# The inverse root's guess in the norms from logarithm and exponential, with a table load placed by hand

## What is computed

```python
def rms_norm(x, g):
    xf = x.astype(jnp.float32)
    y = xf * lax.rsqrt(jnp.mean(xf * xf, axis=-1, keepdims=True) + EPS)
    return (y * g.astype(jnp.float32)).astype(x.dtype)

def mixer_block(h, ...):
    xn = rms_norm(h, norm1_g)
    proj = xn @ w_in                      # fq fk fv ff cq ckv krope sq sk sv gates
    fq, fk = rms_norm(fq per head, fox_q_g), rms_norm(fk per head, fox_k_g)
    log_decay = jnp.cumsum(jax.nn.log_sigmoid(ff + fox_forget_b), axis=1)
    out_a = causal_block_attention(fq, fk, fv, log_decay)
    q = rms_norm(rms_norm(cq, mla_q_a_g) @ mla_w_q_up, mla_q_g)      # then rope
    kv = rms_norm(ckv, mla_kv_a_g) @ mla_w_kv_up
    k = rms_norm(k of kv and krope, mla_k_g)                         # then rope
    out_b = causal_block_attention(q, k, v_mla)
    sq, sk = rms_norm(sq per head, swa_q_g), rms_norm(sk per head, swa_k_g)
    out_c = sliding_window_attention(sq, sk, sv, swa_sinks, slopes)
    merged = sum over branches of sigmoid(gates) * (branch @ w_branch)
    return h + merged @ w_o

def conv_ffn(h, norm2_g, w_up, conv_w, conv_b, w_down):
    u = rms_norm(h, norm2_g) @ w_up       # convolution over 3 positions: gate, val
    return h + (jax.nn.silu(gate) * val) @ w_down
```

## Time and profile before

| | before |
|---|---|
| median of 3 runs | 2309.89 us |
| the profiled execution | 2311.74 us |
| its span | 2309.6 us |
| PE busy | 2064.9 us, 89% |
| DVE busy | 1293.0 us, 56% |
| ACT busy | 683.7 us, 30% |
| POOL busy | 882.9 us, 38% |

### The profile page before, as it was taken

One profiled execution on the slowest core, in us unless ns is written; L12 is line 12 of the kernel. 1 busy time (PEld: TensorE's weight loads), 2 busy tenths in 40 slices (PEclk: granted clock), 3 DMA queues, 4 the chain that ended last, 5 costly groups with the idle time before them and its releaser, 6 DMA issues.

```text
span 2309.6 us, 36668 instructions
## 1 busy us (share of the span) xinstructions
PE 2064.9 (89%) x15052; PEld 1945.4 (84%) x15052; DVE 1293.0 (56%) x2300; ACT 683.7 (30%) x1221; POOL 882.9 (38%) x494
## 2 busy tenths in 40 slices
PE   4999877878889999999979998878788899999999
PEld 3888776777779999999968887767777799999999
DVE  7565656466646565562266656564666565666511
ACT  3434332433331222220024343324343322222200
POOL 6444332232333344444464444322223334444443
PEclk9999988889889999999989999888898999999999
DMA  3111110111113333223221111111111132333333
GB/s 127 47 54 57 55 37 28 37 37 47 46 46 102 92 92 87 88 91 97 88 91 56 56 49 54 37 28 37 38 45 46 46 111 85 95 97 92 93 100 92
DMA packets 44794, 156.27 MB, mean 68 GB/s; under 512 B 5010, under 2 KB 5266, under 8 KB 44628
## 3 DMA queue, kind: packets, MB, share of 16 engines
q1 hardware_dynamic: 44484, 153.71, 22.2%
q10 hardware_dynamic: 144, 0.22, 0.0%
HBM read 149.58 MB, written 4.26 MB: 67 GB/s over the span
## 4 chain that ended last, share of the span: by engine, by line
PE 72%; DVE 18%; issue 5%; ACT 3%; POOL 1%; DMA 0%; DVEq 0%; ACTq 0%; POOLq 0%
PE ps L1156 20%; PE ps L1159 19%; PE ps L1161 19%; PE ps L1364 4%; PE ps L1166 3%; DVE osum L1731 2%; DVE rstd L1447 2%; PE ps L1312 1%; DVE ps L1701 1%; PE ps L1274 1%; DVE guess L1443 1%; DVE yq L1602 1%; DVE wh L1428 1%; DVE q L1575 1%; PE ps L1318 1%
## 5 line engine op out<-in xcount | busy, mean ns | idle before, releaser
L773 POOL TENSOR_TENSOR wl<-raw,wh 128x1024 fp32r<-128x1024 f32 x270 | 648.0, 2400 | 911.9 <-DVE wh L1428 905.9
L1156 PE MATMUL ps<-xh,wh 128*128 128x264 f32 (+1 forms) x2880 | 830.2, 309 | 35.8 <-DVE xl L1506 16.2
L1159 PE MATMUL ps<-xl,wh 128*128 128x264 f32 (+1 forms) x2880 | 781.9, 291 | 0.0
L1156 PEld LDWEIGHTS ps<-xh,wh 128*128 128x128 f32 x2880 | 564.1, 196 | 60.4 <-DVE xl L1506 18.9
L1161 PE MATMUL ps<-xh,wl 128*128 128x264 f32 (+1 forms) x2880 | 596.8, 289 | 0.0
L1159 PEld LDWEIGHTS ps<-xl,wh 128*128 128x128 f32 x2880 | 563.9, 196 | 13.1 <-issue 5.0
L1161 PEld LDWEIGHTS ps<-xh,wl 128*128 128x128 f32 x2880 | 463.7, 195 | 0.0
L1428 DVE CAST wh<-raw 128x1024 fp32r<-128x1024 f32 x270 | 199.9, 741 | 188.8 <-PE ps L1156 170.4
L1723 DVE TENSOR_TENSOR ps<-ps,cst 128x128 f32<-128x128 f32 (+6 forms) x240 | 69.6, 295 | 239.4 <-PE ps L1318 163.5
L1159 PE MATMUL ps<-al,wh 128*128 128x264 f32 (+1 forms) x704 | 185.0, 283 | 0.0
L1156 PE MATMUL ps<-ah,wh 128*128 128x264 f32 (+1 forms) x704 | 183.6, 283 | 0.0
(11 more groups left out here) (174 smaller groups left out, 3300.7 us busy)
## 6 DMA issues: line engine op xcount, KB each, us to landing
raw<-weights SPq DMA_DIRECT2D x270, 512.0 KB, 3.6
h<-tokens SPq DMA_DIRECT2D x4, 528.0 KB, 6.0
h<-tokens SPq DMA_DIRECT2D x8, 264.0 KB, 5.3
residual<-h SPq DMA_DIRECT2D x8, 264.0 KB, 4.7
h<-residual SPq DMA_DIRECT2D x8, 264.0 KB, 5.1
out<-h SPq DMA_DIRECT2D x8, 256.0 KB, 4.8
cst<-constants SPq DMA_DIRECT2D x1, 1008.0 KB
extra<-positions SPq DMA_DIRECT2D x17, 4.1 KB
```

Source lines behind the costliest of these rows:

```text
L773: nc.gpsimd.tensor_tensor(wl[c % SPLIT][:, :], raw[:, c % RAW, :], wh[c % SPLIT][:, :].bitcast(F32), ALU.subtract).then_inc(s_lo, 1)
L1156: a = nc.tensor.matmul(out, a_hi, x_hi[:, sl], start=first, stop=False)
L1159: nc.tensor.matmul(out, a_hi, x_lo[:, sl], start=False, stop=False)
```

## The change

The guess is no longer one function. Ln of the mean plus epsilon is taken, then Exp of -0.5 times that, then the Square as before: one ACTIVATE and one wait more per norm. A flag, `table["now"]`, follows which table is loaded as the program is written: `logarithms()` asks by name for the table that holds both Ln and Exp if the flag doesn't say so already, and it is called at the start of `rsqrt_guess` (behind the waits of lines 1016, 1017, 959 to 961, 1117 and 1118) and ahead of the decay's Exp. The flag is cleared at each Tanh and behind norm 2, since Silu follows. In front of Tanh and Silu the compiler puts its loads as before.

```diff
+            table = {"now": None}
+
+            def logarithms():
+
+                if table["now"] != "ln":
+                    nc.scalar.preload_act_table_set("natural_log_exp_and_others")
+                    table["now"] = "ln"
+
+            def follows(ins):
+
+                ins.then_inc(act_step.sem, act_step.tick(("a", act_step.n)))
+                act.wait_ge(act_step.sem, act_step.n)
+
             def rsqrt_guess(slot, n):
-                nc.scalar.activation(guess[:, :], full(slot), ACT.Abs_reciprocal_sqrt, scale=1.0 / n,
-                                     bias=epsb[:, 0:1]).then_inc(act_step.sem, act_step.tick(("a", act_step.n)))
-                act.wait_ge(act_step.sem, act_step.n)
+                logarithms()
+                follows(nc.scalar.activation(guess2[:, :], full(slot), ACT.Ln, scale=1.0 / n, bias=epsb[:, 0:1]))
+                follows(nc.scalar.activation(guess[:, :], guess2[:, :], ACT.Exp, scale=-0.5))
                 return nc.scalar.activation(guess2[:, :], guess[:, :], ACT.Square)
...
                             act.wait_ge(act_step.sem, act_step.at("f", l, 0))
+                            logarithms()
                             nc.scalar.activation(fe, fa, ACT.Exp, scale=-1.0).then_inc(
...
+                            table["now"] = None
                             nc.scalar.activation(gate_tile(t.m), full(t.slot), ACT.Tanh, scale=0.5).then_inc(
...
                 rsqrt_guess(1, D).then_inc(guess_ready.sem, guess_ready.tick((l, "n2")))
+                table["now"] = None
```

## The result

The changed kernel takes 2323.72 us, the median of 5 runs (2318.20 to 2326.82); the kernel before, timed beside it, 2308.85 us. The ratio is 1.0059, 95% interval 1.0040 to 1.0078: slower by 14 us (9 to 18). The forecast was 2329 in a range of 2312 to 2342. The profiled execution after is 2318.55 us with a span of 2316.4, so 6.8 us over the one profiled before. It is one of the two shortest of the five, which is why it shows less than the medians do.

The account below looks back on a forecast made before the run. PE was taken as the bound (busy 89% of the span, 72% of the chain). Terms of 9.5 us per layer, 19.0 in all, plus 0.7 once each made 19.7, taken as 19 on 2309.9: 2329 us, range 2312 to 2342.

Parts of the forecast that it names:

- Rival A: At the norms, the explicit load stays ahead of the wait for the statistic: 2313 us; chance 0.13.
- rival B: In the attention stages ACT's queue decides and its total counts: -11.4 us in all, 2298 us; chance 0.08.
- rival C: At the 58 norms the compiler's own loads still come behind the explicit one: some 50 us, 2360; chance 0.02.
- the terms for Fox, the sliding window and norm 1: Per layer: sliding-window shift rows +2.0, Fox queries 2 and 3 +1.1, Fox query 1 -0.3; layer 1's norm 1 +1.95.
- The terms for MLA: Per layer: query 1 -0.6, key 0 +0.65, queries 5 to 7 together +0.6, key 3 +1.95 us.
- MLA key 3: In each layer DVE waits for this key's guess and goes on to PE's scores: +1.95 us.
- terms put at nothing: Norm 2 of both layers, MLA keys 1 and 2, fewer loads ahead of exponentials elsewhere: all costed at nothing.
- The third term put at nothing: Fewer loads ahead of exponentials elsewhere: costed at nothing, as PE doesn't wait there.
- The Tanh term: Three Tanh loads per layer, at 449.56 and two more places: +1.28, 0.7 and 0.8, together +2.8 us per layer.
- The decay term: Decay of layer 1: two loads on the chain vanish, 2.57; query 0's guess takes back 0.67: -1.9 us.
- Link and spared loads: Extra Exp: 0.67 us from statistic to guess per norm, 37.4 us of ACT; 38 fewer loads: 48.8 us of ACT less.
- The signs I named: Profile after: 36 explicit loads, 34 Tanh loads, 58 Exp, ACT near 672 us, PE idle some +19, more DVE waits.

Follow-up runs that it names:

- e1: The changed kernel with the explicit table load asked for ahead of the waits for the statistic: 2307.85 us, ratio 0.9995 against the kernel before.
- e3: The kernel before with its own 54 norm loads made explicit and so put behind the waits, no additional link: 2341.27 us, ratio 1.0131.
- e10: The changed kernel with the load ahead of the waits, except in MLA's queries and keys and the layer's second norm: 2316.64 us, ratio 1.0032.
- e11: The changed kernel with the load ahead of the waits only in MLA's queries and keys and the second norm: 2313.68 us, ratio 1.0021.
- e4: The changed kernel with the gates' Tanh replaced by a Copy, so the 34 Tanh loads vanish: 2323.59 us, ratio 1.0059 against the kernel before.
- e5: The kernel before with the decay's Exp and Ln table named ahead of its wait, and the first guess's table at the start: 2311.96 us, ratio 1.0012.
- e6: e1 with the guess's Ln taken away, Exp reading the sum of squares directly (values wrong): 2296.43 us, ratio 0.9946 against the kernel before.
- e2: The kernel before with one additional Copy activation in the guess's chain, tables and loads untouched: 2331.25 us, ratio 1.0097.
- e8: e1 with Tanh's table asked for ahead of a score tile's wait (only 12 of 34 loads moved), first table at the start: 2309.86 us, ratio 1.0001.
- e9: e1 without the Square and Newton step, VectorE only scaling the guess from Ln and Exp: 2253.31 us, ratio 0.9763 against the kernel before.
- e12: The kernel before, with its old guess, without the Square and Newton step, VectorE only scaling the guess: 2238.62 us, ratio 0.9691.

## Why the prediction held, and which of its terms did not

**The direction and the mechanism held.** The load written behind both waits waits with them: the rows of line 948, e1 and e3 show it. Rival A (the load runs ahead), rival B (ACT's total decides, 2298) and rival C (more loads) are out for the changed kernel. e1 is rival A built on purpose. It was 2313 by my sum and measured 2307.85.

**The size of the place.** Rival A's terms add up to 5.3 us, which I rounded to 5, so between them and my forecast's sum lie 14.4 us, all from where the load stands. Measured: 14.8 (e1 against the changed kernel, 10 to 20). By place, the terms for Fox, the sliding window and norm 1 make (2.0 + 1.1 + 0.3) x 2 + 1.3 = 8.1, and e10 gave 6.2. The terms for MLA make (1.25 + 0.6 + 1.28) x 2 = 6.3, and e11, which has norm 2 as well, gave 8.8. Both differences are within the noise of the two runs. The step at sliding-window query 0 can be read directly. PE's timeline of the changed kernel, as the earlier trace rows:

```profile
230.06 0.18 PE L1328 MATMUL ps<-xq,xk 97*16 97x16 f32 x1 [1.05 <-ACT xq L941]
```

PE waits 1.05 us for the copied row, where I took 1.0. MLA key 3 held too: DVE waited 4.65 us for the guess before, 6.86 after. DVE's timeline of the changed kernel:

```profile
660.79 0.71 DVE L1459 SCALAR_TENSOR_TENSOR guess<-ps,guess 128x528 f32<-128x528 f32 x1 [6.86 <-ACT guess L960]
```

It reaches PE, which waits for that key. PE's timeline before and after:

```profile
666.44 0.36 PE L1274 MATMUL ps<-xk,xq 96*128 96x264 f32 x1 [3.22 <-DVE xk L1641]
```

```profile
667.31 0.56 PE L1290 MATMUL ps<-xk,xq 96*128 96x264 f32 x1 [5.31 <-DVE xk L1657]
```

That is 2.09 more where I took 1.95.

**Two of the terms put at nothing held.** At norm 2 of layer 0 DVE's wait for the guess grows from 4.73 to 6.68 us, the whole 1.95, but PE doesn't notice: from 780 to 796 us it is busy for all 16.00 in both kernels. At MLA key 2 the guess is late by 1.56 us, and the cover of the earlier trace rows gives way for it. DVE's second Newton instruction in the changed kernel:

```profile
590.50 0.75 DVE L1463 SCALAR_TENSOR_TENSOR rstd<-guess,guess 128x528 f32<-128x528 f32 x1
```

It starts later and takes 0.75 us instead of 2.39, and ends at 591.25, where it ended at 592.07 before. The first norm's +0.67 was swallowed in the same way: its second Newton instruction ends at 19.21 in both kernels (18.05 and 1.16 before, 18.50 and 0.71 after). The third term put at nothing, the loads spared ahead of exponentials, failed; it stands below.

**The Tanh term failed at the end, though not in the waits.** I took 2.8 us per layer, 5.6 in all, for three Tanh loads in line. The waits are there: PE's wait behind the Tanh of 449.56 grew from 2.15 us to 3.57 in the changed kernel, 1.42 where I took 1.28, and without any Tanh load PE's idle time is 4.8 us less (e4). But e4 is no faster. What the sum had wrong is the step from a wait to the time: it takes PE's own work as fixed, and in e4's profiled execution the matmuls took 4.9 us more at a lower clock (0.945 in the mean against 0.947). This term is most of what my 19 was too large by.

**The decay term failed.** -1.9 us for the decay of layer 1. ACT's work did come 2.6 us earlier, and e5, which takes the same two loads off the chain, is not faster. My term let DVE and PE follow ACT without loss. Beside POOL's subtraction DVE's first instruction of the decay took 2.26 us instead of 0.70, and PE's wait moved to the next statistic.

**Link and spared loads.** My other terms said that the link and the 38 loads fewer come to about +5, Tanh and decay among it; without these two they come to +1.7. The runs split it: -12.5 us for the loads spared (e6), +11.3 for the link (e1 against e6), +14.8 for the place. The sum is +13.6, the measured ratio's value; it must be, since each step starts where the one before ends, so it is no check. I had written "PE doesn't wait there" of the exponentials' loads; e6 shows that they are worth something, about a quarter of each microsecond of loads. Rival B's total is thus part of the story, and the link takes it away again. The link was worth 22 us in e2, where exponentials still had their loads, and 11 in e1. Between the profiled executions PE's idle time accounts for 15.2 us (e2) and 10.1 (e6), its busy time for 8.3 and 1.3, so more of that difference is PE's busy time (7.0 us) than waits (5.1). Why was not settled: e2's mean granted clock is 0.941 against 0.940 in the kernel before, so it doesn't show the 8.3.

**The signs I named.** Loads 36 and 34, Exp 58, ACT busy 671.2: as said. No row of the kernel before shows which functions share a table, on which my counts rest; the changed kernel's trace shows the 36 and the 34, and no load between the 58 Ln and their Exp. PE's idle time grew by 15.0 us (said: some 19), among it at the shift row and behind the Tanh, where I had placed it. DVE waits for the guess in 13 norms; "far more than 9" was too much.

**The sum as a whole.** I was 5 us high, by terms that partly cancelled: Tanh 5.6 too high, decay 1.9 too low, link and spared loads together 2.9 too high (+1.7 against a measured -1.2). Each of these two is over 10 us by itself, and my working has neither as a sum of its own. That they nearly cancel was luck; the place of the load was not.

## What to carry to other kernels

Ask for a table by name ahead of the wait for the operand, at the point where the engine is idle anyway, and then look in the timeline which side of the wait the load stands on: 36 loads on the wrong side cost 15 us here, though there were 38 fewer of them. A count of loads, or of an engine's busy time, says little for an engine that is busy for 30%: read whose queue stands behind the longer chain, and price a link by taking it out (e6), not only by adding one (e2). When an experiment moves an instruction, look in its trace whether it moved (e8). Before polishing a guess that a Newton step refines, time the kernel without the step (54 to 71 us here), and then measure whether the accuracy bears it.

## What the runs showed of the hardware

**A slow stretch of PE's clock moved with the waits.** The timelines and windows of e5 show it around the decay: a granted clock of 0.50 behind the wait of 3.87 us before, and behind that of 4.96 us in e5. The changed kernel and e4 show what it can cost: 65.41 and 72.23 us for the same work, at a granted clock of 0.92 and 0.83. e9 and e12 show it over a whole execution: equal idle time, 12.6 us apart in busy time, at 0.947 and 0.956. So these two kernels differ by half a per cent with the same idle time in all, and a local gain of 2.6 us (e5) or 4.1 us (e4) in the trace was no forecast of the total.

**VectorE instructions that work on SBUF alone stood still while GpSimd's subtraction ran: 2.39 us instead of 0.71.** In the prediction I took the 2.39 us of a second Newton instruction for a cover that doesn't move. The same meeting at MLA query 0 of layer 0, DVE's timeline of the kernel before:

```profile
429.43 2.38 DVE L1447 SCALAR_TENSOR_TENSOR rstd<-guess,guess 128x528 f32<-128x528 f32 x1
431.85 0.70 DVE L1624 TENSOR_TENSOR q<-rawt,rstd 96x528 f32<-96x528 f32 x1
```

and POOL's:

```profile
428.86 2.39 POOL L773 TENSOR_TENSOR wl<-raw,wh 128x1024 fp32r<-128x1024 f32 x1 [6.35 <-DVE wh L1428]
```

POOL ends at 431.25 and DVE at 431.81. In e9, where the step before has one SBUF operand, DVE's timeline is:

```profile
410.23 0.42 DVE L1462 TENSOR_SCALAR rstd<-guess 128x528 f32<-128x528 f32 x1
410.68 2.78 DVE L1638 TENSOR_TENSOR q<-rawt,rstd 96x528 f32<-96x528 f32 x1
```

and POOL's:

```profile
410.38 2.52 POOL L773 TENSOR_TENSOR wl<-raw,wh 128x1024 fp32r<-128x1024 f32 x1 [6.08 <-DVE wh L1447]
```

POOL ends at 412.90, DVE 0.56 us later, the same 0.56 as before. The one-operand instruction started 0.15 us ahead of POOL's, and takes 0.42 us; the next one, with two, waits for POOL's end and takes 2.78 instead of 0.70. Where POOL was first, one operand was no protection: 1.78 us instead of 0.42. DVE's timeline of e9 in the sliding-window stage, and POOL's:

```profile
217.05 1.78 DVE L1462 TENSOR_SCALAR rstd<-guess 128x528 f32<-128x528 f32 x1
```

```profile
216.14 2.40 POOL L773 TENSOR_TENSOR wl<-raw,wh 128x1024 fp32r<-128x1024 f32 x1 [0.24 <-POOL xq L853]
```

That one ends 0.29 us behind POOL's. So part of what e9 saves on the Newton step moves to the next instruction: the 16 multiplies of line 1638 take 1742 ns in the mean, those of line 1624 before 705. The meetings of the other norms look alike: of the 58 second Newton instructions of the kernel before, the 15 that start while POOL's subtraction runs end 0.56 to 0.58 us behind it, and so does the decay's instruction in e5, 0.56 us behind.

**The activation started right behind its load.** In the changed kernel's Fox query 2 the load of 135.75 ends at 137.03 and Ln starts at 137.04. Where no wait comes between, behind 50 of the 111 loads of the kernel before and 52 of the 73 of the changed one, the activation starts 0.01 or 0.02 us after the load's end, the compiler's loads and the explicit ones alike.

**Between which functions loads stood.** In the kernel before one of 1283 ns stands each of the 52 times that an exponential or a Tanh follows a guess, and each of the 50 times that a guess follows one of them. One stands between the decay's Exp and its Ln, and one between that Ln and the next guess (41.53 and 44.01 in layer 0). None stands where a Tanh and an exponential follow each other, 42 times. In the changed kernel none stands between the 58 Ln and their Exp, nor ahead of an exponential behind a Tanh, 20 times. One stands ahead of each of the 34 Tanh that come behind an Ln with no other Tanh since. Copies, squares and Abs have none ahead of them in either trace, except the very first square (1.15). Of the 4.2 us of idleness ahead of the compiler's 54 loads at the norms 3.27 are one wait, that of the earlier trace rows.
